# Ring order of the first seven loads, and which projection round carries which modulation pieces

## What is computed

```
c_act = silu(c)
mod = c_act @ w_mod[layer] + b_mod[layer]          # one row of 6 x 1024 for each layer
sh1, sc1, g1, sh2, sc2, g2 = split(mod, 6)
xn = rms_norm(h, norm_mix) * (1 + sc1) + sh1
proj = xn @ ret_w_in                                # 1024 x 6144: q, k, v and gate of 4 heads
q, k = rope(q), rope(k)
o = retention(q, k, v)                              # decayed, causal, chunkwise
mix = (silu(g) * normalised(o)) @ ret_w_out
h = h + g1 * mix
h = h + g2 * grouped_top2_moe(modulate(rms_norm(h), sh2, sc2))
# layer 2: latent attention in place of retention (with a shift and scale of its own from w_mod_kv), then the same MoE
```

## Time and profile before

| | us |
|---|---|
| Median of 3 runs (958.05 to 958.41) | 958.27 |
| The profiled execution | 958.6 |
| Its span, first to last instruction | 956.8 |
| TensorE busy in the span | 902.6 (94%) |
| VectorE busy | 388.3 (41%) |
| ScalarE busy | 176.6 (18%) |
| GpSimd busy | 34.6 (4%) |

### The profile page before, as it was taken

The page is one execution under the profiler, slowest core; times in us unless marked ns, Lnnn a source line. Parts: engine busy times, 40 slices in busy tenths (PEclk is TensorE's granted clock), DMA queues, the critical chain, the costliest instruction groups (busy, mean ns, idle before and its releaser), DMA issues.

```text
span 956.8 us, 11788 instructions
## 1 busy us (share of the span) xinstructions
PE 902.6 (94%) x4437; PEld 485.2 (51%) x4438; DVE 388.3 (41%) x729; ACT 176.6 (18%) x321; POOL 34.6 (4%) x43
## 2 busy tenths in 40 slices
PE   6995999999998899999999988998899999999996
PEld 3884444444444454554554556864454554544552
DVE  2848567867824531223321242423531223322223
ACT  2100111212002211212102131322212212112211
POOL 0022000000001000000000003101000000000000
PEclk9998899999999999999999999999999999999999
DMA  9999999998659799699999975435099699099991
GB/s 324 387 349 387 356 385 364 342 382 346 248 193 423 281 412 418 267 424 422 422 422 422 391 276 187 165 133 198 28 407 419 267 423 410 1 358 422 422 376 44
DMA packets 63662, 308.63 MB, mean 323 GB/s; under 512 B 6007, under 2 KB 6138, under 8 KB 38286
## 3 DMA queue, kind: packets, MB, share of 16 engines
q1 hardware_dynamic: 61274, 304.42, 79.7%
q10 hardware_dynamic: 2356, 3.76, 1.2%
HBM read 307.11 MB, written 1.05 MB: 322 GB/s over the span
## 4 chain that ended last, share of the span: by engine, by line
PE 86%; DVE 7%; DMA 2%; issue 2%; ACT 1%; SPq 0%; DVEq 0%; POOL 0%
PE bank L811 13%; PE bank L798 12%; PE bank L829 12%; PE bank L671 12%; PE bank L855 6%; PE bank L709 6%; PE bank L778 6%; PE bank L612 3%; PE bank L1039 3%; DMA ring<-in_w_mod 2%; DVE part L1357 2%; PE bank L821 1%; PE bank L994 1%; PE bank L980 1%; PE bank L933 1%
## 5 line engine op out<-in xcount | busy, mean ns | idle before, releaser
L811 PE MATMUL bank<-ring,arena 128*64 128x256 f32 x1088 | 124.1, 381 | 0.0
L1573 DVE TENSOR_TENSOR arena<-bank,arena 128x256 f32<-128x256 f32 x34 | 21.0, 618 | 240.2 <-PE bank L811 240.2
L1357 DVE SCALAR_TENSOR_TENSOR part<-ring,cpad,part 128x1024 f32<-128x1024 f32 x84 | 108.6, 1293 | 22.3 <-DMA ring<-in_w_mod 17.4
L671 PE MATMUL bank<-ring,xnT 128*128 128x512 f32 x256 | 112.2, 597 | 0.0
L829 PE MATMUL bank<-ring,arena 128*64 128x512 f32 x480 | 108.9, 596 | 0.0
L798 PE MATMUL bank<-ring,arena 128*64 128x512 f32 x480 | 106.3, 596 | 0.5 <-DVE arena L1566 0.5
L811 PEld LDWEIGHTS bank<-ring,arena 128*64 128x64 f32 x1088 | 76.7, 137 | 46.9 <-issue 12.6
L671 PEld LDWEIGHTS bank<-ring,xnT 128*128 128x128 f32 x256 | 48.7, 192 | 61.8 <-issue 61.8
L778 PEld LDWEIGHTS bank<-arena,y 128*128 128x128 f32 x544 | 63.2, 192 | 12.7 <-DVE arena L1555 9.0
L778 PE MATMUL bank<-arena,y 128*128 128x128 f32 x544 | 63.7, 276 | 3.8 <-DVE arena L1555 3.8
L798 PEld LDWEIGHTS bank<-ring,arena 128*64 128x64 f32 x480 | 33.2, 137 | 63.1 <-issue 61.1
(11 more groups left out here) (256 smaller groups left out, 830.1 us busy)
## 6 DMA issues: line engine op xcount, KB each, us to landing
ring<-in_moe_w_up SPq DMA_DIRECT2D x64, 1024.0 KB, 9.1
ring<-in_moe_w_gate SPq DMA_DIRECT2D x56, 1024.0 KB, 9.3
ring<-in_moe_w_down SPq DMA_DIRECT2D x56, 1024.0 KB, 11.3
ring<-in_w_mod SPq DMA_DIRECT2D x48, 1024.0 KB, 12.3
ring<-in_ret_w_in SPq DMA_DIRECT2D x24, 1024.0 KB, 11.7
ring<-in_w_mod_kv SPq DMA_DIRECT2D x8, 1024.0 KB, 13.3
ring<-in_ret_w_out SPq DMA_DIRECT2D x8, 1024.0 KB, 9.2
arena<-in_moe_w_down SPq DMA_DIRECT2D x2, 2048.0 KB, 16.3
```

The lines of the kernel that those rows point to most:

```text
L671: ins = pe.matmul(pair[tt][:], xnT[:, k, tok(tt)], w[:, k, :], start=(k == 0), stop=(k == KT - 1))
L811: ins = pe.matmul(bank[1 + f][e * 64:(e + 1) * 64, 0:256], xgT[:, k, e * 64:(e + 1) * 64], w(2 + e, k)[:, f * 256:(f + 1) * 256], start=(k ...
L1357: ins = dve.scalar_tensor_tensor(o, w[:, k, :], c, o, ALU.mult, ALU.add)
```

## The change

```
-STREAM = [("mod", 0), ("mod", 1), ("win", 0), ("win", 1), ("win", 2), ("mod", 2), ("mod", 3)]
+STREAM = [("mod", 0), ("mod", 1), ("mod", 2), ("win", 0), ("win", 1), ("win", 2), ("mod", 3)]

-MODS_PER_ROUND = (0, 0, 1, 3, 2, 2, 2, 2, 2, 2, 2, 2)
+MODS_PER_ROUND = (1, 0, 1, 1, 2, 2, 3, 2, 2, 2, 2, 2)
```

## The result

The changed kernel took 969.74 us (median of 4 runs, 969.32 to 970.09) against 958.34 for the kernel before on the same chip: a ratio of 1.0115, with a 95% interval of 1.0097 to 1.0132. Slower by 11 us, as forecast (969.2). A second set of runs gave a smaller ratio (see `after_again`).

A forecast was written before the change was run, and what follows sets the result against it. TensorE, busy 94% of the span, was taken as the bound. Terms +3.1 (first pause), +5.4 (second pause) and +2.4 (clock behind it) gave +10.9 us: 969.2 us on the median of 958.27, range 963 to 973.

The forecast's parts named there:

- What bounds the kernel: Whole kernel: TensorE is busy 94% of the span, so only its pauses count.
- The first pause: TensorE's pause moves from behind round 3 to ahead of it, 14.2 us for 11.05: +3.1 us, its half clock unchanged.
- I take 64.3: Landing time of piece 4's load if ScalarE's queued loads pass first; served alone it would be 60.7.
- The second pause: Round 6, three pieces: new 5.4 us TensorE wait for a gate store, plus 2.4 us of half clock behind it.
- From round 7 the two orders are the same, so the shift stays to the end: From round 7 on TensorE releases every load, so the shift of +10.9 us lasts to the kernel's end.
- a start of round 7 less than 8 us later than 153.40: One of three named signs that would show the forecast wrong, at the start of round 7.
- One side sum: Pricing half clock by the Trainium skill's rule, 2.8 us for 3.1, would make the sum about 0.3 us lower.
- clock stays up: Round 6: pause as forecast but no half clock behind it, 0 for 2.4 us: 966.8 us, chance 0.14.
- nothing lands earlier: Piece 4 lands at 66.2 as before, pause ahead of round 3 1.9 us longer: 971.1 us, chance 0.10.
- round 6 costs nothing: VectorE's chain in round 6 stays under 19.2 us, so no new pause there: 961.4 us, chance 0.06.
- starved: Later release of piece 8 makes a block or piece 13 late by about 5 us: 974 us, chance 0.06.
- The faster side: Piece 4 lands by 53.4, so TensorE does not pause ahead of round 3: -6.3 us, 952.0 us, chance 0.04.

The follow-up runs named there:

- after_again: The changed kernel itself run once more, nothing altered, beside the kernel before: 967.26 us, ratio 1.0072 to the kernel before.
- two_in_round6: The changed kernel with the third piece of round 6 moved to round 3: 961.42 us, ratio 1.0023 to the kernel before.
- even_pairs: The changed kernel with pieces spread (0, 0, 0, 2, 2, 2, 2, 3, 2, 3, 2, 2): 948.30 us, ratio 0.9882 to the kernel before.

## Why the prediction was right, and where it was not

**What bounds the kernel: right.** Every version's start of L736 follows TensorE's pauses and the half clock behind them. In no version did TensorE itself wait for a load in rounds 4 to 11; in `two_in_round6` it did so through VectorE.

**The first pause: right in kind, wrong in size.** The step that failed is "I take 64.3": piece 4 landed at 60.7, the other end of my bounds, since SP's queue kept 83 to 100% of the engines from 53 to 56 us. Everything behind it held: 4.7 us for the piece, 2.9 us for each bank, 5.92 for piece 5. The term was +3.1. TensorE could have gone on at 71.03 (0.17 us later than the 70.86 of before), so the pause is 81.60 - 71.03 = 10.6 for 11.05, -0.5, just what I gave for that end. Its half clock, which I kept at 3.1, cost 1.2 us at the gate sum and 1.0 in round 3 (14.96 for 13.98): 2.2, hence -0.9 more. The term was 4.5 us too high.

**The second pause: right.** 5.4 forecast; 154.64 - 148.55 - 0.86 = 5.2 measured. The clock behind it was put at 2.4 and cost 1.2 + 0.9 + 0.5 at the small operations and 0.5 in round 7, 3.1 us. `two_in_round6` and `even_pairs` show that the cause is three pieces in a round that also holds both sums of a gate vector; three pieces alone don't do it (round 7 of `even_pairs`), and both sums in a round of two pieces was not run.

**"From round 7 the two orders are the same, so the shift stays to the end": wrong by 4.0 us.** The order is the same, and nearly so are the waits, but the granted clock is not. The step put the clock in the layers at no change, without a reason; the profiles show 23.8 us of half clock there for 6.8. Its cause stays open.

The sum 10.9 agreed with 10.7 (967.5 less 956.8 of span) because the errors cancelled: -4.5 at the first pause, +0.5 at the second (-0.2 and +0.7), +4.0 in the layers. The prediction named a start of round 7 less than 8 us later than 153.40 as a sign of being wrong, and that came: 159.40 against 153.24, 6.2 us. So the shift of the stage was forecast too long by some 4 us, and the number was hit by luck; the two pauses, their places and their order of size were not luck. One side sum was wrong as well: 2.8 us for the clock in place of 2.4 would raise the sum by 0.4, not lower it by 0.3.

The rivals: "clock stays up" fell (2.07 us for a gate sum at 154.64), "nothing lands earlier" fell (60.7), "round 6 costs nothing" fell (5.2 us), "starved" fell for the changed kernel. The faster side's condition, piece 4 landed by 53.4, was missed by 7 us, even with the late constants out of the way by 5 us; `even_pairs` gets the gain meant there by another way, by leaving the gathers behind round 3.

## What to carry to other kernels

When work is moved in one engine's program, look for the wait that the same list creates in another engine's program: here VectorE had the time for a piece in an earlier round, but its gather became a wait ahead of a whole round of TensorE. Work that passes back and forth through one buffer (sum, store, second sum) should have its two passes in different rounds. And read the clock of stretches that the change doesn't touch, in several executions of both kernels, before a difference of a few us is put down to the change or to chance.

## What the runs showed of the hardware

- The same kernel took 966.6 to 969.7 us (changed kernel, six runs) and 958.2 to 964.1 (kernel before, twenty runs). The two profiled executions of the changed kernel have the same pauses and differ in how long half clock lasts behind one of them (6.8 and 3.4 us at the first router).
- A pause of 3.4 us before a router was followed by half clock in both profiles of the changed kernel and in that of the kernel before; a pause of 1.9 us in the stage (`even_pairs`, round 9) was not. In the changed kernel's layers waits of 1.9 and 2.3 us (up to 330.96 and 595.57) were followed by 3.4 us of half clock each, and the kernel before had none at those places. So the length of the last pause alone doesn't tell whether the clock falls.
- While both queues had work (53 to 56 us of the changed kernel), they moved nearly as many packets each, 94 to 103 per us. SP's packets were larger, so it moved 0.33 to 0.39 MB per us and had 83 to 100% of the transfer engines, ScalarE's queue 8 to 18%.
- VectorE's pass of 1.3 us takes up to 1.63 beside GpSimd's rotary sums: piece 5 takes 5.92 us there (changed kernel) and 5.25 alone (`even_pairs`). GpSimd's sums take 1.70 us then, and 0.72 otherwise.
